# Three stage borders of an encoder layer re-ordered on one core: the first rows, gate/up and down

## The chip, the core and the metric

The kernel runs on one core of a Trainium2 chip. The metric is the device time of one execution in microseconds (us). A core has five engines that run side by side, each through its own list of instructions in order: TensorE (PE in the rows; PEld is its weight load), VectorE (DVE), ScalarE (ACT), GpSimd (POOL) and SyncE (SP), which here only issues transfers (DMA). They wait for each other by semaphores. SBUF is the core's working memory; PSUM, with eight banks of 128 x 512 float32, is where TensorE puts its sums.

## The reference

One layer on 2048 tokens of width 1024, all in float32, then a last RMSNorm:

```python
u = rms_norm(x, norm_mix_g)
q, k, v, b, c, h = split(u @ w_in)              # six parts, 512 wide each
att = diff_attention(q, k, v) + T5 bias         # softmax(s0) - lam * softmax(s1), times v; 4 heads
att = rms_norm(att, subln_g) * (1 - lam_init)
conv = b * short_conv(c * h, conv_w)            # centred, 3 wide
x = x + concat(att, conv) @ w_out
z = rms_norm(x, norm_ffn_g)
hid = silu(z @ w_gate) * (z @ w_up)             # 2816 wide
out = rms_norm(x + hid @ w_down, final_g)
```

The bias of a score depends only on key position minus query position, by 32 buckets, so that one vector of 512 values a head holds all of it.

## The kernel before

Every large product is made of three products of rounded parts: each operand is split into a high part (a rounded copy, made by ACT) and a low part (the rest, made by DVE as a subtraction of two tiles), and PE sums hi x hi, hi x lo and lo x hi. The stages follow one another on PE:

1. **The start.** The 2048 rows come in four blocks of 512 (`sb`), each of four tiles of 128 (`j`). For a tile: `square` on ACT (L745), `mean` on DVE, a power on GpSimd (L682) for 1/sqrt, `scale_x` on DVE (L1084), eight transposes on PE (`turn_u`, L1555), then `split_u` on ACT (L756) and DVE (L1090). Before that PE makes the bias vectors of the four heads (L1538), and ACT copies them out and stores them. `first_product(sb, r)` is 24 matmuls (L1546) for one of three output pieces. Between the first products of a block the next block's tiles are turned. An exponential for lambda (`lam_exp`, L782) stands on ACT ahead of the squares of block 1.
2. **The projections**, then the convolution: for each group of 128 channels three pieces `r` of four blocks.
3. **The attention.** Before its first score is used, ACT fills `window` with the bias: `fill_far` (L836) writes the constant ends and `fill_near` (L832) the middle, which SP loads (`near_stage`, L452).
4. **The output projection**, 16 row tiles `n` in `ORDER`. A tile is normed, turned into `z_turned`, copied to `zt` by ACT (`evacuate_z`, L921), and stored to a DRAM tensor `z_blocks`; for each pair of tiles four sums are made on DVE (`sum_z`, L1328 to L1333) and stored as well (`store_z`, seven stores of 256 KB, L533 and L536).
5. **Gate/up.** A Strassen-like scheme of 7 products (`k` = 0 to 6) over 4 x 4 tiles, in 44 steps: 22 chunks of weights for the first half of the tokens, then 22 for the second. A product is 12 matmuls (L1734; in step 0 L1750). The tokens' parts lie in seven pairs `z_slot[k]`, loaded from `z_blocks` and split by ACT (L928, L932) and DVE (L1314, L1320), 128 x 2048 each. `split_w` splits the weights (L943, L1354); `make_u_2`, `make_u_3`, `make_c_22`, `make_c_21` and `make_c_12` (L1360) read the sums out of PSUM; `hidden` (L1386) gives 128 x 512 of the result, stored by `store_hid` (L586). In the last step of the first half (`gate_up_step(F_CHUNKS - 1, ...)`) all seven pairs are made anew: a raw block waits in one of three `z_stage`, and SP loads block `k` (`load_z_next`, L594) when block `k - 3` has been split. `load_z_next(6)` stands on SP behind `store_hid` of that step's first piece.
6. **Down**, four groups of 22 chunks (L1792), each chunk a hidden tile and a weight tile that are loaded (L640, L642), split by ACT (L1029, L1031) and DVE (L1481, L1484). Ahead of the load of chunk 2 SP issues the four `y_rows` of the group (L634) and the gain.

All orders are written out by hand, and all SP transfers go out on one queue.

## Time and profile before

| | us |
|---|---|
| median of 3 runs | 2781.87 (2779.66 to 2782.27) |
| the profiled execution | 2779.97 |
| its span, first to last instruction | 2778.1 |
| PE busy | 2665.7 (96%) |
| DVE busy | 1511.9 (54%) |
| ACT busy | 1021.9 (37%) |
| GpSimd busy | 501.2 (18%) |

PE is the bound: what it doesn't do between its first and its last instruction is 112 us, spread over the borders between stages and over the attention. The mean granted clock of TensorE over the span was 0.988. In the chain of work that ended last, PE's gate/up and down products take 15% and 17% of the span by themselves.

### The profile page before, as it was taken

The numbers are of one execution on the slowest core, as the hardware profiler recorded it, in microseconds if no ns is written. First come the engines' busy times: TensorE is split into PE (matmuls) and PEld (weight loads), VectorE is DVE, ScalarE is ACT, GpSimd is POOL, SyncE is SP. The second block draws the span as 40 slices with busy tenths as digits, with TensorE's granted clock in tenths as the row PEclk, the third lists the DMA queues.
The fourth block names the chain that finished last, engine by engine and source line by source line (L and its number), as shares of the span: only waits on it lengthen the run. The fifth ranks groups of instructions, "written<-read, shape, count | busy, mean of one in ns | idle before, by whom it ended". The sixth has DMA issues, their size and how long they took to land. (4 is left out here: it accounts for less than half of the span.)

```text
span 2778.1 us, 34594 instructions
## 1 busy us (share of the span) xinstructions
PE 2665.7 (96%) x12280; PEld 2184.4 (79%) x12280; DVE 1511.9 (54%) x2203; ACT 1021.9 (37%) x1429; POOL 501.2 (18%) x343
## 2 busy tenths in 40 slices
PE   7999999979999999989989999989999999999997
PEld 5788888857777777778868888878888878888886
DVE  5311122258878887854466666676666643434343
ACT  5210000047667676742243333343333323323232
POOL 1000000047777777720000000000000000000000
PEclk9999999999999999999989999999999999999999
DMA  5542111223131221047762222252222235556563
GB/s 171 147 124 87 57 38 38 61 64 71 28 75 46 68 57 31 20 157 224 229 219 76 83 91 72 87 174 91 72 87 88 75 120 152 170 175 207 146 203 116
DMA packets 257359, 298.29 MB, mean 107 GB/s; under 512 B 15200, under 2 KB 175456, under 8 KB 257280
## 3 DMA queue, kind: packets, MB, share of 16 engines
q1 hardware_dynamic: 254400, 287.83, 35.1%
q0 software_dynamic: 2304, 8.39, 0.7%
q8 instruction: 46, 0.75, 0.1%
q10 hardware_dynamic: 576, 1.05, 0.1%
q14 instruction: 33, 0.27, 0.0%
HBM read 212.28 MB, written 84.93 MB: 107 GB/s over the span
## 5 line engine op out<-in xcount | busy, mean ns | idle before, releaser
L1734 PE MATMUL banks<-z_hi,w_hi 128*128 128x512 f32 x1204 | 469.9, 390 | 8.4 <-ACT p L947 5.5
L1734 PE MATMUL banks<-z_hi,w_lo 128*128 128x512 f32 x1204 | 469.4, 390 | 0.0
L1734 PE MATMUL banks<-z_lo,w_hi 128*128 128x512 f32 x1204 | 469.3, 390 | 0.0
L1546 PE MATMUL projected<-u_t_hi,w_part_hi 128*128 128x512 f32 (+1 forms) x768 | 300.3, 391 | 5.3 <-DVE u_t_lo L1090 2.6
L1546 PE MATMUL projected<-u_t_lo,w_part_hi 128*128 128x512 f32 (+1 forms) x768 | 299.3, 390 | 0.0
L1546 PE MATMUL projected<-u_t_hi,w_part_lo 128*128 128x512 f32 (+1 forms) x768 | 299.3, 390 | 0.0
L697 POOL TENSOR_TENSOR exp<-exp,exp 128x2048 f32<-128x2048 f32 x64 | 295.6, 4618 | 5.3
L1734 PEld LDWEIGHTS banks<-z_hi,w_hi 128*128 128x128 f32 x1204 | 226.8, 188 | 56.8 <-issue 5.9
L1734 PEld LDWEIGHTS banks<-z_lo,w_hi 128*128 128x128 f32 x1204 | 226.8, 188 | 47.0
L1734 PEld LDWEIGHTS banks<-z_hi,w_lo 128*128 128x128 f32 x1204 | 226.6, 188 | 47.2
L842 ACT ACTIVATE exp<-exp,neg_max 128x2048 f32<-128x2048 f32 x128 | 257.3, 2010 | 15.3 <-DVE neg_max L1228 14.4
L726 POOL TENSOR_TENSOR y_rstd<-y_mean,neg_half 128x1 f32<-128x1 f32 x16 | 8.7, 546 | 1343.4 <-DVE y_mean L1496 1343.4
L943 ACT ACTIVATE w_hi<-w_sum 128x512 fp32r<-128x512 f32 x176 | 111.3, 633 | 319.1 <-PE banks L1734 307.3
L1792 PE MATMUL banks<-down_hi,hid_hi 128*128 128x512 f32 x704 | 217.7, 391 | 3.9 <-DVE down_lo L1484 3.9
L1792 PE MATMUL banks<-down_lo,hid_hi 128*128 128x512 f32 x704 | 217.7, 390 | 0.0
L1792 PE MATMUL banks<-down_hi,hid_lo 128*128 128x512 f32 x704 | 217.4, 390 | 0.0
L852 ACT ACTIVATE a_t_hi<-tile_turned 128x512 fp32r<-128x512 f32 x256 | 148.7, 601 | 158.1 <-PE tile_turned L1622 157.8
L1240 DVE TENSOR_TENSOR a_t_lo<-tile_turned,a_t_hi 128x512 fp32r<-128x512 f32 x256 | 172.1, 687 | 54.3 <-ACT a_t_hi L852 54.2
L1604 PE MATMUL scores<-k_sum,q_part_hi 128*128 128x512 f32 x512 | 179.4, 432 | 18.7 <-DVE half_min L1228 10.3
L1481 DVE TENSOR_TENSOR hid_lo<-hid_raw,hid_hi 128x512 fp32r<-128x512 f32 x88 | 60.9, 693 | 247.6 <-ACT hid_hi L1029 247.6
L1228 DVE CUSTOM_DVE_ANT_0 exp<-scores,window,half_min 128x1024 f32<-128x1024 f32 x128 | 163.9, 1280 | 31.7 <-PE scores L1604 26.1
L1029 ACT ACTIVATE hid_hi<-hid_raw 128x512 fp32r<-128x512 f32 x88 | 55.6, 632 | 324.2 <-PE banks L1792 313.4
(143 smaller groups left out, 4420.9 us busy)
## 6 DMA issues: line engine op xcount, KB each, us to landing
down_raw<-in_w_down SPq DMA_DIRECT2D x88, 512.0 KB, 4.4
gate_raw<-in_w_gate SPq DMA_DIRECT2D x44, 512.0 KB, 4.7
up_raw<-in_w_up SPq DMA_DIRECT2D x44, 512.0 KB, 5.6
hidden_t<-hid_stage SPq DMA_DIRECT2D x88, 256.0 KB, 2.7
hid_raw<-hidden_t SPq DMA_DIRECT2D x88, 256.0 KB, 3.7
w_raw<-in_w_in SPq DMA_DIRECT2D x24, 512.0 KB, 5.3
projected_t<-stage SPq DMA_DIRECT2D x48, 256.0 KB, 2.5
z_stage<-z_blocks SPq DMA_DIRECT2D x11, 1024.0 KB, 5.8
```

The lines of the kernel that those rows point to most:

```text
L697: nc.gpsimd.tensor_tensor(exp_0[:, slot_0], exp_0[:, slot_0], exp_1[:, slot_1], ALU.add).then_inc(mixed_ready, 1)
L842: nc.scalar.activation(rows, rows, ACT.Exp, scale=-1.0, bias=neg_max[:, t % 2, part:part + 1], accum_out=exp_sum[:, part, t % 16:t % 16 + ...
L852: nc.scalar.activation(dst, turned_bank(h, t, index), ACT.Copy).then_inc(group_hi, 1)
L943: nc.scalar.activation(w_slot[k][0][:, :, :], src, ACT.Copy).then_inc(w_hi_ready_2, 1)
L1029: nc.scalar.activation(hid_part[slot][0][:, :], hid_raw[:, slot], ACT.Copy).then_inc(f_hi_ready, 1)
L1228: nc.vector.tensor_tensor_reduce(out=rows[:, half * HALF:(half + 1) * HALF], in0=scores[:, unit % 2], in1=window[:, window_slice(t, half)] ...
L1240: nc.vector.tensor_tensor(parts[1][at], turned_bank(h, t, index), parts[0][at].bitcast(FP32), ALU.subtract).then_inc(group_lo, 1)
L1481: nc.vector.tensor_tensor(hid_part[slot][1][:, :], hid_raw[:, slot], hid_part[slot][0][:, :].bitcast(FP32), ALU.subtract).then_inc(f_lo_re ...
L1546: last = nc.tensor.matmul(projected[:, bank * BANK:(bank + 1) * BANK], w_part[w][:, r, kt], u_t[u][:, kt, rows], start=(kt == 0 and n == 0 ...
L1604: last = nc.tensor.matmul(scores[:, unit % 2, b * BANK:(b + 1) * BANK], q_part[n][:, (t // 4) % 2, part, t % 4 * P:(t % 4 + 1) * P], k_sum ...
L1734: last = nc.tensor.matmul(c_bank[BANK_OF[k]], w_slot[k][w][:, kt], z_slot[k][z][:, kt], start=(kt == 0 and t == 0 and k in (0, 1, 3, 4)), ...
L1792: last = nc.tensor.matmul(y_banks[j][:, c * BANK:(c + 1) * BANK], hid_part[slot][h][:, j * P:(j + 1) * P], down_part[slot][w][:, c * BANK: ...
```

## The change

- **Start.** SP issues all four tiles of block 0 at once: two go to `x_tile`, two to `early`, which are parts of the last block's columns of `u_t_lo`, in pieces of 512 bytes. The small loads and the gain go out on ACT's queue. PE makes bias 0 first, bias 1 behind the four turns, and biases 2 and 3 behind `first_product(0, 0)`; `turn_u(1, 0)` follows those.
- **Attention.** SP loads the bias's middle right behind the start, and ACT fills the window when four products of the convolution are still to come; the high parts of the weights lie in other slots (`HI_SLOT`).
- **Gate/up.** GpSimd makes the four sums of the last two pairs, and `z_lo` of block 5 in the first half and of blocks 1, 3 and 5 in the second (`Z_ON_POOL`). SP issues the loads of blocks 4 to 6 and the last rows ahead of `store_z(6)`. PSUM banks, the places of several tiles and the orders on ACT and DVE are other.
- **Down.** DVE splits chunk 0 ahead of `make_c_12`, and ACT splits chunk 1 ahead of `silu_second`.

```diff
         lam_exp = placed(210144, "lam_exp", [P, 2])
 
+        early_rows = placed(20480 + 65536, "early_rows", [P, KT, SEQ])
+        early = [early_rows[:, :, 3 * BANK + n * P:3 * BANK + (n + 1) * P] for n in range(4)]
+        bias_vec = [early[2 + h // 2][:, 4 * (h % 2):4 * (h % 2) + 4] for h in range(HEADS)]
+
+        HI_SLOT = (1, 2, 0)
...
+
+        Z_ON_POOL = ((5,), (1, 3, 5))
+
+        def z_count(half, k, on_pool):
+
+            return sum((j in Z_ON_POOL[n]) == on_pool for n in range(half + 1) for j in range(7 if n < half else k + 1))
+
+        def wait_z(engine, half, k):
+            if k in Z_ON_POOL[half]:
+                engine.wait_ge(z_lo_pool, z_count(half, k, True))
+            else:
+                engine.wait_ge(z_lo_ready, z_count(half, k, False))
+
...
-            load_x(0, 0)
-            load_x(0, 1)
-            sp.dma_start(onehot[:, :], bucket_onehot).then_inc(rel_loaded, 16)
-            sp.dma_start(rel_sb[:, :], rel_bias).then_inc(rel_loaded, 16)
-            sp.dma_start(mix_gain[:, :], norm_mix_g[0:1, :].to_broadcast([P, D])).then_inc(gain_loaded, 16)
-            load_weights(0, 0, 0)
-            load_x(0, 2)
-            load_weights(0, 1, P)
-            load_x(0, 3)
-            load_weights(0, 2, 2 * P)
+            for j in range(2):
+                sp.dma_start(x_tile[:, j], x_rows[j * P:(j + 1) * P, :]).then_inc(x_loaded[j], 16)
+            for j in range(2):
+                sp.dma_start(early[j], x_rows[(2 + j) * P:(3 + j) * P, :].rearrange("p (k q) -> p k q", q=P)).then_inc(early_loaded[j], 16)
+            for r in range(3):
+                load_weights(0, r, r * P)
...
+            sp.wait_ge(bias_stored, 16 * HEADS)
+            load_near(0)
...
+                if n % 2 == 0 and 2 <= n < N_ROWS - 2:
                     store_z(n // 2 - 1)
                 if n == N_ROWS - 1:
 
@@ -570,6 +588,8 @@
                     for k in (4, 5, 6):
                         sp.dma_start(z_slot[k][1][:, :, :].bitcast(FP32), z_dram[0, k].rearrange("k p t -> p k t")).then_inc(z_placed[k - 4], 16)
                 store_rows(n)
+                if n == N_ROWS - 1:
...
-                sp.wait_ge(z_lo_ready, 7 + k - 2)
+                if k >= 3:
+                    wait_z(sp, 1, k - 3)
+                elif k == 0:
+                    wait_z(sp, 0, 3)
                 sp.wait_ge(z_stored[1], 16 * 28)
-                sp.wait_ge(rows_stored[k % 2], 16 * (N_ROWS // 2))
...
 
-            for n in range(N_ROWS):
+            def sum_z(pair):
+                pool.wait_ge(zt_ready, 2 * pair + 2)
+                pool.wait_ge(z_stored[(pair - 1) // 4], 16 * 7 * ((pair - 1) % 4 + 1))
+                b11, b21, b12, b22 = zt[:, 0, 0:4], zt[:, 0, 4:8], zt[:, 1, 0:4], zt[:, 1, 4:8]
+                t1, t2, t3, t4 = (zt_sum[:, n] for n in range(4))
+                nc.gpsimd.tensor_tensor(t1, b12, b11, ALU.subtract).then_inc(zt_sum_ready, 1)
+                nc.gpsimd.tensor_tensor(t3, b22, b12, ALU.subtract).then_inc(zt_sum_ready, 1)
+                pool.wait_ge(zt_sum_ready, 4 * pair + 1)
+                nc.gpsimd.tensor_tensor(t2, b22, t1, ALU.subtract).then_inc(zt_sum_ready, 1)
+                pool.wait_ge(zt_sum_ready, 4 * pair + 3)
+                nc.gpsimd.tensor_tensor(t4, b21, t2, ALU.subtract).then_inc(zt_sum_ready, 1)
+
+            def split_z(half, k):
+                pool.wait_ge(z_hi_ready, 7 * half + k + 1)
+                raw = z_stage[k % 3][:, :, :] if half else z_slot[k][1][:, :, :].bitcast(FP32)
+                nc.gpsimd.tensor_tensor(z_slot[k][1][:, :, :], raw, z_slot[k][0][:, :, :].bitcast(FP32), ALU.subtract).then_inc(z_lo_pool, 1)
+
+
+            for n in range(N_ROWS - 1):
                 rsqrt_row(n)
+            sum_z(N_ROWS // 2 - 2)
+            rsqrt_row(N_ROWS - 1)
+            for k in Z_ON_POOL[0]:
+                split_z(0, k)
+            sum_z(N_ROWS // 2 - 1)
+
+            for k in Z_ON_POOL[1]:
+                split_z(1, k)
...
+            act.dma_start(rel_sb[:, :], rel_bias).then_inc(rel_loaded, 16)
+            act.dma_start(onehot[:, :], bucket_onehot).then_inc(rel_loaded, 16)
+            act.dma_start(mix_gain[:, :], norm_mix_g[0:1, :].to_broadcast([P, D])).then_inc(gain_loaded, 16)
+            for j in range(4):
+                square(0, j)
+            keep_bias(0)
+            split_u(0, 0)
+            split_u(0, 1)
             split_weights(0, 0)
-            for j in range(4):
-                split_u(0, j)
-                if j < 2:
-                    square(0, j + 2)
-                    split_weights(0, j + 1)
+            split_u(0, 2)
+            split_u(0, 3)
+            keep_bias(1)
+            split_weights(0, 1)
+            split_weights(0, 2)
+            keep_bias(2)
+            keep_bias(3)
             act.wait_ge(lam_summed, 2)
             nc.scalar.activation(lam_exp[:, :], lam_sum[:, :], ACT.Exp).then_inc(lam_exped, 1)
...
-            act.wait_ge(piece_ready, 12 * QKV_TRIPLES + 12 * CONV_GROUPS)
+
+            act.wait_ge(piece_ready, 12 * QKV_TRIPLES + 12 * CONV_GROUPS - 4)
             act.wait_ge(w_lo_ready, 3 + 24)
+            fill_near(0)
             fill_far(0, 1)
-            fill_near(0)
             fill_far(0, 0)
...
+                if n == N_ROWS - 1:
+
+                    act.wait_ge(o_summed, N_ROWS)
+                    split_z(0, 3, 0, 4)
                 square_rows(n)
                 if n + 2 < N_ROWS:
                     split_m(n + 2)
-                if n >= 1:
+                if 1 <= n < N_ROWS - 1:
                     evacuate_z(n - 1)
...
-
-            act.wait_ge(o_summed, N_ROWS)
-            split_z(0, 3, 0, 4)
-            split_w(0, 0, 3, True)
             copy_p_0(0)
-            split_w(0, 0, 4, True)
+            for k in range(3, 7):
+                split_w(0, 0, k, True)
+            split_placed_z(4)
+            evacuate_z(N_ROWS - 2)
+            split_placed_z(5)
             evacuate_z(N_ROWS - 1)
+            split_placed_z(6)
 
             act.wait_ge(rows_stored[0], 16 * (N_ROWS // 2))
             act.wait_ge(rows_stored[1], 16 * (N_ROWS // 2))
-            for k in range(5, 7):
-                split_w(0, 0, k, True)
-            split_placed_z(4)
-            split_placed_z(5)
+            silu_first(0)
             split_w(1, 1, 0)
             split_w(1, 1, 1)
-            split_placed_z(6)
-
-            act.wait_ge(z_stored[1], 16 * 28)
-            silu_first(0)
             for k in range(2, 7):
                 split_w(1, 1, k)
             silu_second(0)
...
             split_down(0, 0, 0, False)
+            split_down(0, 1, 1, False)
             silu_second(STEPS - 1)
-            act.wait_ge(product_ready, 7 * STEPS)
-            split_down(0, 1, 1, False)
...
+            mean(0, 0)
             dve.wait_ge(gain_loaded, 16)
-            norm_block(0, lambda r: split_weights(0, r))
+            scale_x(0, 0)
+            mean(0, 1)
+            scale_x(0, 1)
+            mean(0, 2)
+            mean(0, 3)
+            scale_x(0, 2)
+            split_u(0, 0)
+            scale_x(0, 3)
+            split_u(0, 1)
+            split_weights(0, 0)
+            split_u(0, 2)
+            split_u(0, 3)
+            split_weights(0, 1)
+            split_weights(0, 2)
...
+                if n == N_ROWS - 1:
+                    split_z(0, 3, 0)
                 norm_rows(n)
-                if n % 2 == 0 and n >= 2:
+                if n % 2 == 0 and 2 <= n < N_ROWS - 2:
                     sum_z(n // 2 - 1)
...
-            split_z(0, 3, 0)
+            make_u_2(0)
             split_w(0, 0, 3)
-            make_u_2(0)
-            for k in range(4, 7):
-                split_w(0, 0, k)
+            split_w(0, 0, 4)
             split_placed_z(4)
-            sum_z(N_ROWS // 2 - 1)
+            split_w(0, 0, 5)
             make_u_3(0)
-            split_placed_z(5)
+            split_w(0, 0, 6)
+            split_placed_z(6)
+            make_c_22(0)
             sum_weights(1, 1, 0)
             split_w(1, 1, 0)
-            make_c_22(0)
             split_w(1, 1, 1)
-            split_placed_z(6)
             sum_weights(1, 1, 1)
             split_w(1, 1, 2)
 
-            dve.wait_ge(z_stored[1], 16 * 28)
+            dve.wait_ge(rows_stored[0], 16 * (N_ROWS // 2))
+            dve.wait_ge(rows_stored[1], 16 * (N_ROWS // 2))
...
-            gate_up_step(F_CHUNKS - 1, 1, lambda k: split_z(1, k, k % 3))
+            gate_up_step(F_CHUNKS - 1, 1, lambda k: None if k in Z_ON_POOL[1] else split_z(1, k, k % 3))
...
             hidden(STEPS - 1, 0)
+            split_down(0, 0, 0)
             make_c_12(STEPS - 1)
             hidden(STEPS - 1, 1)
-            split_down(0, 0, 0)
             split_down(0, 1, 1)
...
+
+            pe.wait_ge(rel_ready, 1)
+            spread_bias(0)
+            pe.wait_ge(identity_ready, 3)
             for j in range(4):
                 turn_u(0, j)
+            spread_bias(1)
+            pe.wait_ge(bias_out, 2)
+            first_product(0, 0)
+            spread_bias(2)
+            spread_bias(3)
+            turn_u(1, 0)
+            turn_u(1, 1)
+            pe.wait_ge(bias_out, 4)
+            first_product(0, 1)
+            turn_u(1, 2)
+            turn_u(1, 3)
             pe.wait_ge(bias_out, 2 * HEADS)
-            with pe.Fori(0, SB - 1) as sb:
+            first_product(0, 2)
+            with pe.Fori(1, SB - 1) as sb:
...
-            pe.wait_ge(zt_ready, N_ROWS - 1)
+            pe.wait_ge(rows_added, N_ROWS)
```

ACT at the start, where the biases are copied out (`stage<-projected`, in the changed kernel `early_rows<-projected`) and the lambda exponential is made. Before:

```order
L771 ACTIVATE bias_edges<-projected 128x2
L774 DMA bias_vectors<-stage 128x512
L739 ACTIVATE w_part_hi<-w_raw 128x1024
L756 ACTIVATE u_t_hi<-u_turned 128x8x128
L745 ACTIVATE conv_y,sumsq<-x_tile 128x1024
L739 ACTIVATE w_part_hi<-w_raw 128x1024
L756 ACTIVATE u_t_hi<-u_turned 128x8x128
L745 ACTIVATE conv_y,sumsq<-x_tile 128x1024
L739 ACTIVATE w_part_hi<-w_raw 128x1024
L756 ACTIVATE u_t_hi<-u_turned 128x8x128 x2
L782 ACTIVATE lam_exp<-lam_sum 128x2
L745 ACTIVATE conv_y,sumsq<-x_tile 128x1024 x2
```

Changed:

```order
L788 ACTIVATE w_part_hi<-w_raw 128x1024 x2
L823 ACTIVATE early_rows<-projected 128x4x128
L824 ACTIVATE bias_edges<-projected 128x2
L826 DMA bias_vectors<-early_rows 512x1x128
L823 ACTIVATE early_rows<-projected 128x4x128
L824 ACTIVATE bias_edges<-projected 128x2
L826 DMA bias_vectors<-early_rows 512x1x128
L845 ACTIVATE lam_exp<-lam_sum 128x2
L801 ACTIVATE conv_y,sumsq<-x_tile 128x1024 x2
L817 ACTIVATE stage<-projected 128x512
```

The copies of biases 2 and 3 have moved from the front of the list to right ahead of the exponential and of block 1's two squares.

SP at the end of the output projection (`z_lo` are the loads of blocks 4 to 6, `z_blocks<-zt` and `z_blocks<-zt_sum` the stores of a pair). Before:

```order
L533 DMA z_blocks<-zt 128x4x128 x3
L536 DMA z_blocks<-zt_sum 128x4x128 x4
L527 DMA rows_x<-rows 128x1024
L571 DMA z_lo_103<-z_blocks 128x4x512
L571 DMA z_lo_105<-z_blocks 128x4x512
L571 DMA z_lo_107<-z_blocks 128x4x512
L527 DMA rows_x<-rows 128x1024
L554 DMA gate_raw_158<-in_w_gate 128x8x128
L554 DMA up_raw_160<-in_w_up 128x8x128
L533 DMA z_blocks<-zt 128x4x128 x3
L536 DMA z_blocks<-zt_sum 128x4x128 x4
```

Changed:

```order
L545 DMA rows_x<-rows 128x1024
L589 DMA z_lo_104<-z_blocks 128x4x512
L589 DMA z_lo_106<-z_blocks 128x4x512
L589 DMA z_lo_108<-z_blocks 128x4x512
L545 DMA rows_x<-rows 128x1024
L551 DMA z_blocks<-zt 128x4x128 x3
L554 DMA z_blocks<-zt_sum 128x4x128 x4
L572 DMA gate_raw_159<-in_w_gate 128x8x128
L572 DMA up_raw_161<-in_w_up 128x8x128
L551 DMA z_blocks<-zt 128x4x128 x3
L554 DMA z_blocks<-zt_sum 128x4x128 x4
```

The seven stores of pair 6 have moved behind the three loads and the last rows. On ACT the copy into `zt` that waits for them now stands between the high parts of blocks 4 and 5 (`z_hi_103`, `z_hi_105`):

```order
L995 ACTIVATE z_hi_103<-z_lo_104 128x2048
L984 ACTIVATE zt<-banks 128x1024
L995 ACTIVATE z_hi_105<-z_lo_106 128x2048
L984 ACTIVATE zt<-banks 128x1024
L995 ACTIVATE z_hi_107<-z_lo_108 128x2048
L1015 ACT_TABLE_LOAD
L1015 ACTIVATE silu_156<-banks 128x512
```

Before, it stood ahead of all three. GpSimd from the last pairs' sums on, before:

```order
L700 TENSOR_TENSOR head_rstd<-head_mean,neg_half 128x4 x2
L716 TENSOR_TENSOR row_rstd<-row_mean,neg_half 128x1 x16
L726 TENSOR_TENSOR y_rstd<-y_mean,neg_half 128x1 x4
L730 DMA out<-y_rows 128x1024 x4
L726 TENSOR_TENSOR y_rstd<-y_mean,neg_half 128x1 x4
```

Changed:

```order
L739 TENSOR_TENSOR row_rstd<-row_mean,neg_half 128x1
L756 TENSOR_TENSOR z_lo_106<-z_lo_106,z_hi_105 128x2048
L746 TENSOR_TENSOR zt_sum<-zt 128x512
L747 TENSOR_TENSOR zt_sum<-zt 128x512
L749 TENSOR_TENSOR zt_sum<-zt,zt_sum 128x512
L751 TENSOR_TENSOR zt_sum<-zt,zt_sum 128x512
L756 TENSOR_TENSOR z_lo_98<-z_stage_149,z_hi_97 128x2048
L756 TENSOR_TENSOR z_lo_102<-z_stage_148,z_hi_101 128x2048
L756 TENSOR_TENSOR z_lo_106<-z_stage_150,z_hi_105 128x2048
```

The last three of these are blocks 1, 3 and 5 of the second half; DVE's list has lost the same three (of the first kernel's rows `z_lo_97`, `z_lo_101` and `z_lo_105`). DVE at blocks 1 and 2 of that step in the changed kernel:

```order
L1386 TENSOR_TENSOR z_lo_96<-z_stage_148,z_hi_95 128x2048
L1432 TENSOR_TENSOR u_152<-banks,p_151 128x512
L1426 TENSOR_TENSOR w_lo_137<-w_sum,w_hi_136 128x512
L1419 TENSOR_TENSOR w_sum<-gate_raw_158,up_raw_160 128x512
L1421 TENSOR_TENSOR w_sum<-gate_raw_158,w_sum 128x512
L1426 TENSOR_TENSOR w_lo_139<-gate_raw_158,w_hi_138 128x512
L1386 TENSOR_TENSOR z_lo_100<-z_stage_150,z_hi_99 128x2048
L1432 TENSOR_TENSOR u_153<-banks,u_152 128x512
L1426 TENSOR_TENSOR w_lo_141<-w_sum,w_hi_140 128x512
```

Between blocks 0 and 2 stand four instructions of 128 x 512 that read two tiles of SBUF (`w_lo_137`, the two `w_sum`, `w_lo_139`); `u_153`, for which the sixth product waits, follows block 2.

## Rows read from the trace of the kernel before

**Rows 1.** The page: busy time, share of the span, instructions, by engine.

```profile
PE 2665.7 (96%) x12280; PEld 2184.4 (79%) x12280; DVE 1511.9 (54%) x2203; ACT 1021.9 (37%) x1429; POOL 501.2 (18%) x343
```

**Rows 2.** Waits of PE: awaited engine and line; total us, times, longest.

```profile
PE banks L1734 <- ACT p L947: 5.5, 1, 5.5
...
PE banks L1750 <- DVE z_lo L1320: 5.3, 1, 5.3
...
PE banks L1792 <- DVE down_lo L1484: 3.9, 1, 3.9
```

**Rows 3.** Timeline of PE at the start (start, us, instruction, idle before).

```profile
7.38 7.19 PE L1538 MATMUL projected<-onehot,rel_wide 32*128 32x512 f32 x8 [7.38 <-DVE rel_wide L1067]
...
25.84 1.97 PE L1555 MATMUL u_turned<-identity,u_tile 128*128 128x128 f32 x8 [1.55 <-DVE u_tile L1084]
...
30.38 0.79 PE L1546 MATMUL projected<-u_t_hi,w_part_hi 128*128 x1 [2.58 <-DVE u_t_lo L1090]
...
37.33 1.91 PE L1555 MATMUL u_turned<-identity,u_tile 128*128 128x128 f32 x16
...
39.00 0.48 PE L1546 MATMUL projected<-u_t_hi,w_part_hi 128*128 x1
...
44.54 1.03 PE L1555 MATMUL u_turned<-identity,u_tile 128*128 128x128 f32 x8
```

**Rows 4.** Timeline of ACT at the start.

```profile
30.50 0.20 ACT L782 ACTIVATE lam_exp<-lam_sum 128x2 f32<-128x2 f32 x1 [1.64 <-DVE lam_sum L1131]
```

**Rows 5.** Timelines of DVE and POOL there, two squares later.

```profile
32.02 0.55 POOL L682 TENSOR_TENSOR rstd<-mean_eps,neg_half 128x1 f32<-128x1 f32 x1 [9.06 <-DVE mean_eps L1077]
...
33.09 1.27 DVE L1084 SCALAR_TENSOR_TENSOR u_tile<-x_tile,rstd,mix_gain 128x1024 f32<-128x1024 f32 x1
...
33.26 1.52 POOL L682 TENSOR_TENSOR rstd<-mean_eps,neg_half 128x1 f32<-128x1 f32 x1 [0.69 <-DVE mean_eps L1077]
```

**Rows 6.** The page: the long GpSimd additions of the attention.

```profile
L697 POOL TENSOR_TENSOR exp<-exp,exp 128x2048 f32<-128x2048 f32 x64 | 295.6, 4618 | 5.3
```

**Rows 7.** Timelines of ACT and DVE where the attention begins.

```profile
577.23 0.52 ACT L832 ACTIVATE window<-near_stage 128x384 f32<-128x384 f32 x1 [3.77 <-DMA near_stage<-bias_vectors]
...
577.79 1.23 DVE L1228 CUSTOM_DVE_ANT_0 exp<-scores,window 128x1024 f32<-128x1024 f32 x1 [4.48 <-ACT window L832]
```

**Rows 8.** Timelines of SP, ACT and PE where gate/up begins.

```profile
1409.86 2.57 SPq L571 DMA_DIRECT2D z_lo<-z_blocks  x3
...
1425.05 0.63 ACT L943 ACTIVATE w_hi<-up_raw 128x512 fp32r<-128x512 f32 x1 [7.03 <-issue]
...
1446.31 0.47 PE L1734 MATMUL banks<-z_hi,w_hi 128*128 128x512 f32 x1
```

**Rows 9.** Engines and transfers in that stretch (the windows view).

```profile
1404.00:1424.00 20.00, 16.73 (x68) 13.05 (x68) 10.54 (x13) 7.22 (x9) 1.08 (x2) 0.83 1.06 356
```

**Rows 10.** Timelines of DVE, PE, SP and ACT between the halves.

```profile
1837.69 2.28 DVE L1314 TENSOR_TENSOR z_lo<-z_stage,z_hi 128x2048 fp32r<-128x2048 f32 x1
...
1843.43 0.50 PE L1734 MATMUL banks<-z_hi,w_hi 128*128 128x512 f32 x1 [2.47 <-DVE u L1360]
...
1850.33 0.69 DVE L1386 TENSOR_TENSOR hid_stage<-up,silu 128x512 f32<-128x512 f32 x1
...
1851.51 0.37 SPq L594 DMA_DIRECT2D z_stage<-z_blocks  x1
...
1857.77 1.91 ACT L928 ACTIVATE z_hi<-z_stage 128x2048 fp32r<-128x2048 f32 x1 [7.16 <-DMA z_stage<-z_blocks]
```

**Rows 11.** Timelines of SP, ACT, DVE and PE where the down product begins.

```profile
2279.66 1.87 SPq L634 DMA_DIRECT2D y_rows<-rows_x  x4
...
2290.73 0.63 ACT L1029 ACTIVATE hid_hi<-hid_raw 128x512 fp32r<-128x512 f32 x1 [10.75 <-DMA hid_raw<-hidden_t]
...
2293.03 1.23 DVE L1484 TENSOR_TENSOR down_lo<-down_raw,down_hi 128x1024 fp32r<-128x1024 f32 x1 [0.88 <-ACT down_hi L1031]
...
2294.41 0.64 PE L1792 MATMUL banks<-down_hi,hid_hi 128*128 128x512 f32 x2
```

More of the change, by code:

```diff
@@ L113, in build @@
         x_loaded = [sem(f"x_loaded_{i}") for i in range(2)]
+        early_loaded = [sem(f"early_loaded_{i}") for i in range(2)]
         w_hi_ready = sem("w_hi_ready")
@@ L1083, in scale_x @@
                     dve.wait_ge(turned, 4 * sb + j + 1)
-                nc.vector.scalar_tensor_tensor(u_tile[:, j % 2], x_tile[:, j % 2], rstd[:, j:j + 1],
-                                               mix_gain[:, :], ALU.mult, ALU.mult).then_inc(u_ready, 1)
+                scaled_x, rows, gain = u_tile[:, j % 2], x_tile[:, j % 2], mix_gain[:, :]
+                if isinstance(sb, int) and sb == 0 and j >= 2:
+                    scaled_x, rows, gain = scaled_x.rearrange("p (k q) -> p k q", q=P), early[j - 2], gain.rearrange("p (k q) -> p k q", q=P)
+                nc.vector.scalar_tensor_tensor(scaled_x, rows, rstd[:, j:j + 1], gain, ALU.mult, ALU.mult).then_inc(u_ready, 1)
             def split_u(sb, j):
@@ L1535, in _, with spread_bias @@
             pe.sem_inc(turned, 2)
-            pe.wait_ge(rel_ready, 1)
-            for h in range(HEADS):
+            def spread_bias(h):
                 nc.tensor.matmul(projected[:, h * BANK:(h + 1) * BANK], rel_wide[:, h], onehot[:, :],
                                  start=True, stop=True).then_inc(bias_mm, 1)
-            pe.wait_ge(identity_ready, 3)
             def product(bank, r, rows):
```

81 lines of the change are left out of this document (39 added, 42 removed).

## The prediction

> **What bounds the kernel now.** I read the page's busy shares first: PE is busy for 2665.7 of 2778.1 us [rows 1], so a gain can only come out of the 112 us in which it isn't, or out of its clock. Then the waits of PE: three single waits of 5.5, 5.3 and 3.9 us stand at the borders that the change touches [rows 2]. Then the timelines there. The first product starts at 30.38 and ends at 37.33, when the next block's tiles are ready to be turned; the second starts at 39.00 [rows 3]. The attention's first score waits 4.48 us on DVE for ACT's window, and ACT waited for the load of its middle [rows 7]. Gate/up comes into its loop at 1446.31 [rows 8], after a stretch with a granted clock of 0.83 and the transfers full at 356 GB/s [rows 9]. Between the halves block 6 arrives late [rows 10], and down starts against its own third chunk [rows 11]. So there are five places, and each is one term.
>
> **1. The start.** Chain of the four tiles, now without a second round of loads: the four tiles, the gain and one weight are 3 MB; at 356 GB/s [rows 9], I put the gain's landing near 7 us and the first scaled tile at 9.5. Behind it DVE has three more scalings (1.27 each, [rows 5]), four low parts and one weight's, which I take at the same size: 8 x 1.2 = 9.7, and some 3 us in which it waits for a turn (1.97, [rows 3]) and ACT's copy (1.0). The first product then starts at about 22.2, 8.2 ahead of 30.38, and ends at E = 29.2 if it needs its 6.95 us again. But the eight turns behind it no longer find their tiles. Biases 2 and 3 now stand behind this product on PE: 7.19 us for 8 instructions [rows 3] is 0.9 each; the same kind of instruction shows half speed there (8 turns in 1.97 against 16 in 1.91 at 37.33), so at full speed the two biases take 1.8. ACT copies them (some 1 us for the second, with its store's issue), then comes the lambda exponential at E + 3.0, then the squares. From the exponential to the end of the first scaling it is 33.09 + 1.27 - 30.50 = 3.9 us [rows 4, 5]; the second is scaled behind the power's end at 34.78, so 1.3 later, at 36.05, or 5.6 behind the exponential. Its turn ends at E + 8.6 + 1 to 2 = 38.8 to 39.8, against 39.00. The 8 us are given back here, and PE has idled for 5 us, behind which products run at half clock for a while (the 0.83 over 20 us of rows 9 is such a stretch and cost 3.4 us). The next load of x hangs on the first scaling, at E + 6.9 = 36.1 instead of 34.4. I take +1.5; from -2 (E at 26, clock kept) to +4 (the 512-byte pieces load slowly).
>
> **2. The attention's entry.** The window is written under products, whose engine has nothing to do with it; ACT idles there. The wait of 4.48 goes [rows 7]; late next is the score itself, about 0.4 us behind the last convolution piece. With PE no longer idle, its scores 3 and 4 aren't slowed: a few tenths more. I take -4.6, from -3.5 to -5.5. What hangs behind moves with it: the stores of the last convolution piece have to land before score 3, with some 1 us to spare.
>
> **3. Gate/up's entry.** The three loads of blocks 4 to 6 (1 MB each) go out when the projection ends, 4 us ahead of 1409.86 [rows 8]. But the copy of tile 14 into `zt`, which waits for the stores of pair 6, now stands ahead of block 5's high part on ACT, and these stores (7 x 256 KB) have moved behind the loads and the last rows. The transfers are full and go in line: the last rows, issued at 1412.5 behind the loads, held ACT until 1425.05 (the wait put down to "issue", [rows 8]). The same bytes in another order: the line's last member ends when it did, so the stores land at about 1425.0. Then 1.0 for the copy, 1.9 for block 5's high part (as in [rows 10]) and its low part on GpSimd. That is an addition of 128 x 2048, 4.62 us [rows 6]: 1432.6. Products 0 to 4 are done by then; 5 and 6 follow, 12 matmuls each of some 0.227 (24 take 5.5 from 39.00 to 44.54, [rows 3]), the first twelve and a few more at half clock (1.2 GHz), 8.5 in all: 1441.1 against 1446.31. I take -5.3; from -3 to -13, the latter if the stores overtake the loads, since block 5 is then ready when PE wants it.
>
> **4. Between the halves.** DVE loses three low parts of 2.28 [rows 10], GpSimd gets them at 4.62 [rows 6]. PE waited 2.47 us for a sum behind two of them, which would go. It doesn't count if DVE is otherwise free: product 2 of the new half waits for a copy on ACT behind block 6's high part, whose load SP issues at 1851.51, behind the store of the piece that DVE makes at 1850.33 [rows 10]. That piece comes behind block 4, which comes behind block 1's low part. With GpSimd's 4.62 in place of DVE's, which can start at 1835.5, block 1 ends at 1840.1, where DVE ended it at 1839.97 [rows 10], so without any hindrance this term is 0.
> But GpSimd and DVE hinder each other when both read. Row: the power takes GpSimd 0.55 us, and 1.52 when DVE has started a scaling (two tiles read from SBUF) 0.17 earlier [rows 5]; 1.52 is the 1.1 of the scaling's rest and 0.45. In the attention GpSimd's 64 additions take 4.62 beside DVE, whose instructions there take one operand from PSUM [rows 6, 7]. What the row shows one way I expect the other way: who has started keeps the second reader out to its end. Then: GpSimd takes block 1 at 1835.5, when its high part is there, and DVE's next weight part waits until 1840.1. Four instructions of 128 x 512 (0.6) and block 2 (2.2) end at 1844.9, and the sum for product 5 at 1845.4, 2.0 behind 1843.43. GpSimd takes block 3 at 1844.8, to 1849.4; DVE's next weight part stands, and block 4 ends at 1853.4. GpSimd takes block 5, to 1858.0, and the piece behind (0.69, two SBUF tiles) ends at 1858.7 instead of 1851.0. Its store and the load of block 6 go out 7.6 us later, and so does everything behind 1857.77. Bounds 0 and +9; I take +7.6, since the one row there is on it shows full exclusion.
> The Trainium skill (SBUF — State Buffer, section "Who interferes with whom") says the same of both directions: a DVE instruction with two SBUF inputs contends with a GpSimd instruction that reads SBUF, and whoever starts first blocks the other for the whole instruction. By that rule the term is +7.6; this trace agrees for GpSimd's side (0.55 to 1.52) and shows nothing of DVE's.
>
> **5. Down's entry.** DVE has chunk 0 ready 3.3 us earlier, and PE's wait of 3.9 [rows 2] shrinks to 0.6. But chunk 2 was only just in time: its low part ends at 2294.3, and PE takes it at 2294.41 without a wait [rows 11]. Its load stands behind the four `y_rows` from 2279.66 on, 2 MB, and landed at 2290.73. They in turn stand behind the store of the last hidden piece, which the two low parts (0.6 and 1.2) put ahead of `make_c_12` push back by 0.6. So PE is done with chunks 0 and 1 at 2288.7 (48 x 0.227 from 2277.8), waits 6 us, and starts chunk 2 at 2294.9, now at half clock for some 5 us: -0, +0.5 and +2.2, so +2.7, from 0 to +3.5.
>
> Sum: +1.5 - 4.6 - 5.3 + 7.6 + 2.7 = +1.9 us. On the profiled execution's 2779.97 (span 2778.1 and 1.9 around it) that is 2781.9; the median of the runs is 1.9 above it, so 2783.8. 0.2% of the median is 5.6 us, about what a measurement of this kernel tells from no change.
>
> **The rivals.**
> - *No exclusion the other way.* DVE reads on beside GpSimd, term 4 is 0: 2783.8 - 7.6 = 2776.2. For it: 4.62 beside a DVE that is busy for most of the attention; against it: those DVE instructions read one SBUF tile, and the 1.52.
> - *The stores of pair 6 overtake the loads.* Then block 5 is ready when PE comes to it, and term 3 is -13: 2783.8 - 7.7 = 2776.1. Against it: the last rows' 12.6 us behind the same loads [rows 8].
> - *Slower: the first rows come late.* The early tiles travel in 512-byte pieces beside the gain and the weights. If they take twice the 1.5 us each that 356 GB/s gives, E is 3 later, everything to the second product hangs on E (term 1), and the first projection's later turns with it: +4 in place of +1.5, and with term 5 and term 4 at their upper ends (0.8 and 1.4 more), 2788.5. It decides once E is beyond 31.
> - *The work moved to GpSimd does what it says, and PE's clock stays up at all five borders:* rival one and terms 1 and 5 at their lower ends, -3.5 and -2.7: 2770.
>
> **How the numbers follow.** Forecast 0.45, of which faster by 0.2% 0.04, within 0.33, slower 0.08. No exclusion 0.24: 0.13 faster, 0.11 within, since 2776.2 lies on the bound. Overtaking 0.10: 0.06 and 0.04. Late rows 0.14, all slower. Everything well 0.07, faster. Faster 0.30, same 0.48, slower 0.22. The range leaves out half of the last case and the ends of the slow one: 2771 to 2790; the forecast's own is 2779 to 2789.
>
> **What would show it.** Term 1: the first product near 22, a wait of some 5 us on PE for `u_tile` behind biases 2 and 3, and the second product near 39 all the same. Term 2: no wait for the window. Term 3: ACT waits for a store (`z_blocks<-zt_sum`) near 1425 and PE for GpSimd's `z_lo`, about 10 us. Term 4: DVE instructions with two SBUF inputs that last 3 to 5 us or start late beside GpSimd's 4.62, and block 6's load behind them; were DVE's rows there 0.69 and 2.28 as before, rival one is true. Term 5: a PE wait of 6 us at chunk 2 instead of 3.9 at chunk 0. The forecast is wrong if PE finds its tiles behind the first product, or if block 5 is split before 1425.

## The result and the profile after

| | before | after |
|---|---|---|
| median of 20 runs, us | 2777.98 (2775.04 to 2782.27) | 2783.48 (2778.42 to 2785.10) |
| the profiled execution | 2779.97 | 2783.90 |
| its span | 2778.1 | 2782.1 |

The ratio is 1.0019, with a 95% interval of 1.0013 to 1.0025: slower by 0.13 to 0.25%, with the point estimate just inside the 0.2% that I called no change. The forecast was 2783.8. That it is met to 0.3 us is partly luck: I added 1.9 to a level of 2781.87, and the median of 20 runs of before is 3.9 lower. The honest comparison is of differences: 1.9 forecast, 3.9 between the two profiled executions, 5.5 between the medians. The profiled execution of before is 2.0 above its median and that of after 0.4 above, so some 1.6 of the 5.5 stand in neither trace.

The page's busy times say nothing of this; PE is even busy for less [rows 1]:

```profile
PE 2664.3 (96%) x12280; PEld 2182.8 (78%) x12280; DVE 1514.3 (54%) x2191; ACT 1021.5 (37%) x1429; POOL 536.9 (19%) x355
```

The waits of PE do [rows 2] (awaited engine and line; total us, times, longest):

```profile
PE banks L1822 <- ACT p L1010: 9.6, 2, 8.8
PE banks L1838 <- issue: 9.5, 1, 9.5
PE u_turned L1627 <- DVE u_tile L1147: 9.1, 4, 5.5
...
PE banks L1880 <- DVE down_lo L1557: 6.1, 2, 5.6
PE banks L1822 <- DVE u L1432: 4.3, 1, 4.3
```

Single waits of 8.8, 9.5, 5.5, 5.6 and 4.3 stand where 5.5, 5.3, 3.9 and 2.5 stood before: the waits have not gone, they have moved.

To see what each place is worth, compare one instruction of the steady stretch behind it in both traces. Two such pairs, before and after: the first long addition on GpSimd behind the attention's entry, then the silu of the last but one gate/up step, behind the border between the halves.

```profile
588.61 4.55 POOL L697 TENSOR_TENSOR exp<-exp,exp 128x2048 f32<-128x2048 f32 x1
...
2247.23 0.60 ACT L952 ACTIVATE silu<-banks 128x512 f32<-128x512 f32 x1 [2.09 <-PE banks L1734]
```

```profile
587.13 4.54 POOL L720 TENSOR_TENSOR exp<-exp,exp 128x2048 f32<-128x2048 f32 x1
...
2248.54 0.60 ACT L1015 ACTIVATE silu<-banks 128x512 f32<-128x512 f32 x1 [2.09 <-PE banks L1822]
```

At 587 us after is 1.48 early, at 2248 it is 1.31 late. Read so at every border:

| place (term) | after minus before, in the steady stretch behind it | the term: difference to the row above | predicted |
|---|---|---|---|
| start (1) | +3.23 (a convolution piece, 117.01 against 113.78) | +3.2 | +1.5 |
| attention's entry (2) | -1.60 (12 tiles of the output projection, all alike) | -4.8 | -4.6 |
| gate/up's entry (3) | -5.45 (19 steps of the first half, all alike) | -3.9 | -5.3 |
| between the halves (4) | +1.30 (20 steps of the second half) | +6.8 | +7.6 |
| down's entry (5) | +3.97 (all chunks from the seventh on) | +2.7 | +2.7 |
| sum | | +4.0 | +1.9 |

These are single executions, one of each kernel. Kernels whose code is the same up to a border differ there as well: by up to 1.3 us in the output projection, and at gate/up's entry, where the transfers decide, the term lay between -1.8 and -4.3 in the six traces that have this entry unchanged (after and the first, second, fourth, fifth and eighth experiment). Term 4 is steadier: 6.0 to 7.3 in the five traces that have GpSimd's part there unchanged.

**The start** [rows 3 to 5], rows of PE, ACT and DVE:

```profile
30.81 1.98 PE L1611 MATMUL projected<-onehot,rel_wide 32*128 32x512 f32 x4
38.27 3.54 PE L1627 MATMUL u_turned<-identity,u_tile 128*128 128x128 f32 x16 [5.48 <-DVE u_tile L1147]
41.56 0.48 PE L1618 MATMUL projected<-u_t_hi,w_part_hi 128*128 128x512 f32 x1
```

```profile
34.35 0.20 ACT L845 ACTIVATE lam_exp<-lam_sum 128x2 f32<-128x2 f32 x1 [0.53 <-ACT bias_edges L824]
```

Biases 2 and 3 follow the first product at 30.81, ACT comes to the exponential at 34.35, and the first turn waits 5.48 us for its tile. The second product starts at 41.56 (before 39.00).

**The attention's entry** [rows 7]. The first score on DVE waits 0.60 for PE; the wait of 4.48 for the window is gone.

```profile
577.15 1.23 DVE L1300 CUSTOM_DVE_ANT_0 exp<-scores,window 128x1024 f32<-128x1024 f32 x1 [0.60 <-PE scores L1692]
```

**Gate/up's entry** [rows 8]: the copy of tile 14 on ACT waits for the stores of pair 6, block 5 is made behind it on ACT and GpSimd, and PE waits 9.53 for it.

```profile
1423.90 1.02 ACT L984 ACTIVATE zt<-banks 128x1024 f32<-128x1024 f32 x1 [10.38 <-DMA z_blocks<-zt_sum]
1424.83 1.90 ACT L995 ACTIVATE z_hi<-z_lo 128x2048 fp32r<-128x2048 f32 x1
```

```profile
1426.80 4.51 POOL L756 TENSOR_TENSOR z_lo<-z_lo,z_hi 128x2048 fp32r<-128x2048 f32 x1 [15.61 <-ACT z_hi L995]
```

```profile
1431.41 0.76 PE L1838 MATMUL banks<-z_hi,w_hi 128*128 128x512 f32 x1 [9.53 <-issue]
...
1439.84 0.39 PE L1822 MATMUL banks<-z_hi,w_hi 128*128 128x512 f32 x1
```

"issue" names nobody here. GpSimd's row ends at 1431.31, 0.1 ahead of the matmul, and the matmul reads the block that it writes, so I take it as the releaser; the third experiment bears that out.

**Between the halves** [rows 10], DVE, then GpSimd in the same 20 us, then SP and PE behind them. These are the rows that decide the case:

```profile
1830.43 4.73 DVE L1426 TENSOR_TENSOR w_lo<-w_sum,w_hi 128x512 fp32r<-128x512 f32 x1
...
1836.89 2.28 DVE L1386 TENSOR_TENSOR z_lo<-z_stage,z_hi 128x2048 fp32r<-128x2048 f32 x1
...
1839.69 4.46 DVE L1426 TENSOR_TENSOR w_lo<-w_sum,w_hi 128x512 fp32r<-128x512 f32 x1
...
1844.68 0.67 DVE L1426 TENSOR_TENSOR w_lo<-w_sum,w_hi 128x512 fp32r<-128x512 f32 x1
1845.28 2.28 DVE L1386 TENSOR_TENSOR z_lo<-z_stage,z_hi 128x2048 fp32r<-128x2048 f32 x1
...
1848.24 4.33 DVE L1458 TENSOR_TENSOR hid_stage<-up,silu 128x512 f32<-128x512 f32 x1
```

```profile
1829.99 4.63 POOL L756 TENSOR_TENSOR z_lo<-z_stage,z_hi 128x2048 fp32r<-128x2048 f32 x1 [390.30 <-ACT z_hi L991]
1838.38 5.22 POOL L756 TENSOR_TENSOR z_lo<-z_stage,z_hi 128x2048 fp32r<-128x2048 f32 x1 [3.77 <-ACT z_hi L991]
1846.99 5.03 POOL L756 TENSOR_TENSOR z_lo<-z_stage,z_hi 128x2048 fp32r<-128x2048 f32 x1 [3.39 <-ACT z_hi L991]
```

```profile
1853.05 0.39 SPq L616 DMA_DIRECT2D z_stage<-z_blocks  x1
```

```profile
1862.10 0.76 PE L1822 MATMUL banks<-z_hi,w_hi 128*128 128x512 f32 x1 [8.83 <-ACT p L1010]
```

The same DVE instruction takes 0.67 alone and 4.73 if GpSimd's began 0.44 earlier: it ends some 0.55 behind GpSimd's, so it has stood still until about then. The same shows the other way round: GpSimd's second and third row begin while a low part of DVE (2.28) is under way, 0.8 and 0.6 ahead of its end, and last 5.22 and 5.03 instead of some 4.6. The load of block 6 goes out at 1853.05 (before 1851.51, with PE 5.45 us ahead), and PE waits 8.83 at 1862.10.

**Down's entry** [rows 11]:

```profile
2279.01 0.73 PE L1880 MATMUL banks<-down_hi,hid_hi 128*128 128x512 f32 x2 [0.59 <-DVE down_lo L1557]
2295.74 1.22 PE L1880 MATMUL banks<-down_hi,hid_hi 128*128 128x512 f32 x2 [5.55 <-DVE down_lo L1557]
```

The wait at chunk 0 is 0.59 (before 3.91), the one at chunk 2 is 5.55 (before none).

### The profile page after: what moved, and what is told of

It reads as the page before. It is cut to its first block and busy times, and to the rows that moved or that the text cites. A ratio compares the mean times of both kernels' runs of the same rounds, so it can differ in the third digit from the quotient of the medians.

```text
span 2782.1 us, 34570 instructions
## 1 busy us (share of the span) xinstructions
PE 2664.3 (96%) x12280; PEld 2182.8 (78%) x12280; DVE 1514.3 (54%) x2191; ACT 1021.5 (37%) x1429; POOL 536.9 (19%) x355
```

## The experiments

All times are medians, ratios are to the kernel before on the same chip. "Back" is against the changed kernel, by the difference of the ratios (1.0019 minus the ratio, times 2778); by the intervals of the two ratios such a difference is known to some 3 us, and to 4 or more in the experiments from the fifth on. Each kernel was timed beside the kernel before, whose median was 2778.43 in the first four, 2779.15 in the next four and 2777.43 in the last two.

**1. The blocks between the halves on DVE again.**

```diff
-        Z_ON_POOL = ((5,), (1, 3, 5))
+        Z_ON_POOL = ((5,), ())
```

> The changed kernel, but the low parts of blocks 1, 3 and 5 between the halves are made by DVE again. Theory (GpSimd and DVE shut each other out when both read two SBUF tiles): in the trace of the changed kernel the stretch between the halves costs 6.75 us against before (the silu copies stand 5.45 us early ahead of it and 1.30 late behind it), and three DVE instructions of 0.68 last 4.73, 4.46 and 4.33 beside GpSimd's additions. With DVE alone these rows are 0.68 again, block 6 is loaded some 5 to 7 us earlier, PE's longest wait there is 5.5 instead of 8.8 and its wait of 4.3 is 2.5; the time falls by 6.8 us. Rival (the place is as late for another reason, the three loads that SP issues or the order on ACT): DVE's rows get short but PE's waits stay, and less than 3 us come back.

2776.66 us, ratio 0.9995 (0.9986 to 1.0004): 6.7 back. In its trace the stretch between the halves costs 8.3 us less than in after (and 1.5 less than in before), PE's waits there are 2.47 and 4.08, and DVE's rows are short:

```profile
1839.60 0.69 DVE L1426 TENSOR_TENSOR w_lo<-w_sum,w_hi 128x512 fp32r<-128x512 f32 x1
...
1846.67 0.69 DVE L1458 TENSOR_TENSOR hid_stage<-up,silu 128x512 f32<-128x512 f32 x1
```

So the loss of term 4 came from GpSimd's part; the rival is out. Reckoned from the steady stretch ahead of it, block 6's load goes out 7.0 later in after than in before, and in this run when it did in before.

**2. The squares ahead of biases 2 and 3** (ACT).

```diff
-            keep_bias(2)
-            keep_bias(3)
             act.wait_ge(lam_summed, 2)
             nc.scalar.activation(lam_exp[:, :], lam_sum[:, :], ACT.Exp).then_inc(lam_exped, 1)
+            square(1, 0)
+            square(1, 1)
+            keep_bias(2)
+            keep_bias(3)
...
-                square(sb + 1, 0)
-                square(sb + 1, 1)
+                if not first:
+                    square(sb + 1, 0)
+                    square(sb + 1, 1)
```

> The changed kernel, but on ACT the lambda exponential and the squares of tiles 0 and 1 of block 1 stand ahead of the copies of biases 2 and 3. Theory (PE's wait of 5.48 us behind the first product hangs on the exponential, which hangs on the biases, which hang on the product): the squares run before 30 us, the turns follow the biases at once, the wait of 5.5 and that of 1.0 go, PE's clock stays up, and the second product starts at 34 to 35 instead of 41.56; the time falls by 6 to 8 us. Rival (the tiles of block 1 are not loaded by then, or the copies of biases 2 and 3, now behind the squares, hold the third product): the second product starts no earlier than 38 and at most 3 us come back.

2777.47 us, ratio 0.9996 (0.9987 to 1.0005): 6.4 back. The exponential runs at 27.44, inside the first product; the 16 turns follow the biases at 32.76 without a wait, and the second product starts at 34.48, 7.1 earlier. The wait of 5.5 was the order on ACT, as the prediction had it.

```profile
32.76 1.97 PE L1630 MATMUL u_turned<-identity,u_tile 128*128 128x128 f32 x16
34.48 0.47 PE L1621 MATMUL projected<-u_t_hi,w_part_hi 128*128 128x512 f32 x1
```

**3. Blocks 4 to 6 ahead of the copies of tiles 14 and 15** (ACT).

```diff
-            split_placed_z(4)
-            evacuate_z(N_ROWS - 2)
-            split_placed_z(5)
-            evacuate_z(N_ROWS - 1)
-            split_placed_z(6)
+            for k in (4, 5, 6):
+                split_placed_z(k)
+            evacuate_z(N_ROWS - 2)
+            evacuate_z(N_ROWS - 1)
```

> The changed kernel, but on ACT the high parts of blocks 4, 5 and 6 stand ahead of the two copies of tiles 14 and 15, the first of which waits 10.4 us for the stores of pair 6. Theory (PE's 9.5 us ahead of product 5 are this wait, then 1.9 for the high part and 4.5 on GpSimd): ACT makes block 5 as soon as it has landed, near 1415, GpSimd has it near 1420, and PE goes from product 4 to 5 without a wait; its clock stays up, so the loop starts near 1428 instead of 1439.8. Some of it is lost to the next wait, since the stores of the rows still land near 1424: I expect 7 to 10 us less in the time. Rival (the loads of the blocks themselves land only near 1422, with the stores, because all transfers share one bandwidth): product 5 starts at 1428 or later and at most 4 us are won.

2775.70 us, ratio 0.9992 (0.9983 to 1.0001): 7.5 back, of which the trace shows 4.8 at this border (after's own -3.9 there is 0.5 better than the mean of the six traces, so the edit may be worth a little more), 1.1 ahead of it, where the code is the same, and 1.3 behind. ACT makes block 5 at 1415.10; product 5 waits 0.49 instead of 9.53. But the loop starts at 1433.50, not near 1428, behind a new wait:

```profile
1423.01 0.47 PE L1837 MATMUL banks<-z_hi,w_hi 128*128 128x512 f32 x1 [0.49 <-DVE u L1431]
...
1433.50 0.79 PE L1821 MATMUL banks<-z_hi,w_hi 128*128 128x512 f32 x1 [4.08 <-DVE w_lo L1425]
```

Ahead of it stand the next weights (`up_raw` landed at 1428.6) and, again, GpSimd; how much of the 4.08 belongs to each isn't separated. One weight part on DVE took 5.11 beside GpSimd's 4.62, and the weight sums took 1.5 to 1.8 instead of 0.69 beside the last pair's sums.

```profile
1417.15 5.11 DVE L1425 TENSOR_TENSOR w_lo<-up_raw,w_hi 128x512 fp32r<-128x512 f32 x1
...
1431.69 1.75 DVE L1425 TENSOR_TENSOR w_lo<-gate_raw,w_hi 128x512 fp32r<-128x512 f32 x1
```

**4. Chunks 2 and 3 ahead of the residual's rows** (SP; DVE's wait for the gain moves to group 1).

```diff
             store_hid(1, STEPS - 1, F_CHUNKS - 1, 0)
+            load_down(0, 2, 0)
             store_hid(1, STEPS - 1, F_CHUNKS - 1, 1)
+            load_down(0, 3, 1)
             sp.wait_ge(product_ready, 7 * STEPS)
             load_y_rows(0)
...
-            with sp.Fori(1, F_CHUNKS // 2) as pair:
+            with sp.Fori(2, F_CHUNKS // 2) as pair:
...
-            dve.wait_ge(out_gain_loaded, 16)
             for group in range(4):
+                if group == 1:
+                    dve.wait_ge(out_gain_loaded, 16)
```

> The changed kernel, but SP loads chunks 2 and 3 of the down product ahead of the four rows of the residual, and DVE waits for the gain only ahead of the second group. Theory (PE's wait of 5.6 us at chunk 2 is the 2.5 MB ahead of its load): chunk 2 is split near 2286, PE doesn't wait behind chunk 1, the clock stays up; the 5.6 go and some 2.5 of half clock: the time falls by 7 to 8 us. Rival (the load of chunk 4, now behind the rows, is late instead): a wait of 3 us or more at chunk 4, and less than 4 us are won.

2775.38 us, ratio 0.9989 (0.9980 to 0.9998): 8.3 back, 8.4 at this border in the trace. Chunk 2's low parts end at 2286.6 and PE runs through; its only wait in down is 0.6. The load of chunk 4 comes late on ACT (a wait of 1.30) but not for PE.

**5. Block 6 loaded ahead of the step's first store** (SP, on top of the first experiment).

```diff
+            load_z_next(6)
             store_hid(0, F_CHUNKS - 1, F_CHUNKS - 1, 0)
-            load_z_next(6)
```

> The kernel of the first experiment (blocks 1, 3 and 5 on DVE again), and SP loads block 6 ahead of the store of the step's first hidden piece instead of behind it. Theory (PE's longest wait there, 4.1 us in that experiment, hangs on this load, which stood behind DVE's piece at 1847.4): the load goes out when block 3 is split, near 1842.5, PE's wait of 4.1 goes and with it some 2 us of half clock: 5 to 6 us less than the first experiment, so 2771. Rival (the transfers are the limit there: the loads of blocks 4 and 5 end only near 1845): block 6 lands near 1850 instead of 1853.5 and 3 us are won at most.

2768.47 us, ratio 0.9968 (0.9956 to 0.9980). The block's high part starts at 1845.11 instead of 1853.52, PE's long wait is gone and this border costs 6.1 less than in the first experiment, 7.7 less than in the kernel before. By the ratios it is 7.5 faster than the first experiment, known to 4 us, so the 5 to 6 that I expected fit, and so does the trace's 6.1. The rival's 3 us don't fit the trace.

**6. All five edits together.**

> All five edits at once: squares ahead of biases 2 and 3, blocks 4 to 6 ahead of the copies of tiles 14 and 15, the blocks between the halves on DVE, block 6 loaded first, chunks 2 and 3 ahead of the rows. If the five borders are independent, the gains add up: against the changed kernel 6.9 + 6.1 + 7.9 + 8.2 from the medians and 5.5 for block 6, 35 in all, so near 2749; against the kernel before, near 0.989. If they aren't (a stage that starts earlier finds its loads late), less: 2755.

2749.19 us, ratio 0.9898 (0.9883 to 0.9913); expected 2749. By the ratios the five edits bring 36.4 one by one and 33.6 together, which is the same within the interval of 0.3%. A steady stretch of some 380 us or more stands between each two borders. It beats both kernels.

**7. GpSimd with one operand.** This kernel leaves out the subtraction in GpSimd's low parts of blocks 5, 1, 3 and 5.

```diff
-  nc.gpsimd.tensor_tensor(z_slot[k][1][:, :, :], raw, z_slot[k][0][:, :, :].bitcast(FP32), ALU.subtract).then_inc(z_lo_pool, 1)
+  nc.gpsimd.tensor_scalar(z_slot[k][1][:, :, :], raw, 1.0, None, ALU.mult).then_inc(z_lo_pool, 1)
```

> The changed kernel, but GpSimd makes its low parts of blocks 5 (first half), 1, 3 and 5 (second half) from one tile: it multiplies the raw block by one instead of subtracting the high part, so this leaves the subtraction out. Theory A (what shuts DVE out is a GpSimd instruction with two operands from SBUF): GpSimd's instructions get shorter and DVE's weight parts beside them last 0.68 again; 5 to 7 us less. Theory B (any GpSimd instruction that reads SBUF shuts out a DVE instruction with two SBUF operands): DVE's rows still last as long as what is left of GpSimd's, near 4 us if it needs as long for one operand as for two.

A single run, so its time (2780.47) says little; in its trace this border costs 4.0 against before, where after has 6.8. DVE and GpSimd between the halves:

```profile
1829.89 3.75 DVE L1426 TENSOR_TENSOR w_lo<-w_sum,w_hi 128x512 fp32r<-128x512 f32 x1
...
1838.17 3.52 DVE L1426 TENSOR_TENSOR w_lo<-w_sum,w_hi 128x512 fp32r<-128x512 f32 x1
...
1845.79 3.52 DVE L1458 TENSOR_TENSOR hid_stage<-up,silu 128x512 f32<-128x512 f32 x1
```

```profile
1829.46 5.37 POOL L756 TENSOR_SCALAR z_lo<-z_stage 128x2048 fp32r<-128x2048 f32 x1 [390.43 <-ACT z_hi L991]
```

Theory A is out: one operand on GpSimd's side shuts DVE out as well. Theory B is nearly right: DVE is held for some 3.5 us from GpSimd's start, but goes on 1.8 ahead of the end of GpSimd's row (1834.83 against 1833.0), where with two operands it stood to the end. GpSimd's rows are rough, so where its reading ends is open.

**8. The window late.**

```diff
-            sp.wait_ge(bias_stored, 16 * HEADS)
-            load_near(0)
...
             store_conv(CONV_GROUPS - 1)
+            sp.wait_ge(bias_stored, 16 * HEADS)
+            load_near(0)
...
-            act.wait_ge(piece_ready, 12 * QKV_TRIPLES + 12 * CONV_GROUPS - 4)
+            act.wait_ge(piece_ready, 12 * QKV_TRIPLES + 12 * CONV_GROUPS)
             act.wait_ge(w_lo_ready, 3 + 24)
-            fill_near(0)
             fill_far(0, 1)
+            fill_near(0)
```

> The changed kernel, but SP loads the bias's middle and ACT fills the window where the kernel before does, behind the last piece of the convolution. Theory (term 2): the wait of 4.5 us ahead of the first exponentials comes back and with it a stretch at a lower clock, so the time rises by 4.8 us, to 2788. Rival (the load of the middle was the whole wait and has its slot earlier in the queue now): less than 2 us.

2787.53 us, ratio 1.0031 (1.0019 to 1.0044): 3.3 slower than the changed kernel by the ratios, 4.0 by the medians and at the output projection in the trace. The waits are those of before, to a tenth: ACT 3.85 for the load, DVE 4.56 for the window. With the load and the filling back in their old places the waits are back, and both hang on the load, so the rival is out by the trace; the time alone, known to 4 us, wouldn't rule it out. An early load with a late filling wasn't run.

**9 and 10. No help from GpSimd, beside all five edits once more.** Experiment 9 has the five edits, and in it DVE also makes block 5 of the first half and the sums of the last two pairs (`Z_ON_POOL = ((), ())`, `sum_z` back on DVE).

> All five edits, and GpSimd helps nowhere: DVE makes the sums of the last two pairs (the last ones behind c22 of the first step) and the low part of block 5 of the first half as well. Theory (beside DVE's subtractions GpSimd gives nothing, since each of its instructions shuts DVE out to its end): with all five edits one DVE weight part of the first step lasted 5.09 beside GpSimd's 4.62 where DVE needs 2.28 for the same block, and four more lasted 1.6 to 1.8 beside the last pair's sums. Without them PE's waits of 0.4 at products 5 and 6 go and the one of 3.5 at the loop's start shrinks to some 2: 2 us less, near 2747. Rival (GpSimd's help is worth its place ahead of the loop): DVE gets 2.3 for the block and 2 x 2.7 for the sums, the last turn and PE's waits get longer, and the time rises by 2 us or more.

> The kernel with all five edits once more, on the same chip as the one without GpSimd's help, so that the two can be compared: 0.990 of the kernel before, near 2749, its loop in gate/up entered behind a wait of 3.5 us.

2745.95 us in 9 (ratio 0.9889, 0.9872 to 0.9905) and 2748.07 in 10 (0.9899, 0.9883 to 0.9916). In 9 the waits of 0.4 at products 5 and 6 are gone, and the loop is entered behind 2.47; the medians say 2 less, but the intervals overlap, and the same entry with unchanged code waited 3.52 in the sixth and 1.68 in the tenth run, which then waits 1.91 more for a copy on ACT. So no gain from GpSimd's help shows here, and no cost either: the difference between the two kernels is known only to some 6 us.

## Why the prediction came out so

- **Term 1, the start: mechanism right, size off** (+3.2 for +1.5). The place is as predicted, and the second experiment shows that ACT's order alone makes it. What was mis-sized is E, the end of the first product: 30.8 instead of 29.2. It started at 22.77 (I said 22.2), but took 8.0 us instead of 6.95: ten of its 24 matmuls last 0.63 and all behind 27.6 last 0.39, where in before five last 0.63. The granted clock is 0.50 over the stretch (the lower level, 1.2 GHz); ahead of the product PE had waited 1.4, 1.8 and 1.3 us for its tiles. Which matmuls fall on the lower clock varies: in seven traces with this start unchanged the product takes 7.3 to 8.5 us, with 8 to 12 of them, and the term is 2.5 to 3.4. I took the 6.95 from a product of before, and priced half clock behind the 5 us wait, but not here. The slower rival's mark, E beyond 31, was missed by 0.2 without its cause: the rows came in time.

```profile
17.70:27.80 10.10, 8.97 (x22) 6.06 (x23) 6.76 (x11) 4.19 (x6) 0.00 (x0) 0.50 0.47 140
```

- **Term 2, the window: right** (-4.8 for -4.6), and the eighth experiment gives 4.2 of it back (in its trace the term is -0.6).
- **Term 3, gate/up: mechanism right, size off** (-3.9 for -5.3; -1.8 to -4.3 over the six traces). The stores held ACT until 1423.90 (I said 1425.0), product 5 came at 1431.41 (1432.6), the loop at 1439.84 (1441.1). My times are on the time axis of before, and after arrives 1.6 early, so up to the loop the sum held to 0.4: -4.9 by then. I stopped it there. Behind it PE lost 1.0 more, 0.8 of it waiting for a copy on ACT. DVE's weight parts of just then lasted 1.77 each beside GpSimd's sums of the last pair: the exclusion that I priced in term 4 had a second place, and I left it out. That it is what made the copy late is argued from the order of the instructions; no run tests it alone.
- **Term 4, the halves: right** (+6.8 for +7.6). Block 6's load went out 7.0 later, where I said 7.6. The first experiment gives back 8.3 in the trace, more than the term: without GpSimd this border is 1.5 shorter than before's, 0.6 by a shorter load of block 6 and 1.0 by fewer matmuls at the lower clock (7 against 12) behind the wait. I had put all but the exclusion at 0; single traces don't say whether that 1.5 is the change or the execution. The one row of before in which a GpSimd power lasted 1.52 beside a DVE scaling carried a rule for the other direction. By the Trainium skill (SBUF — State Buffer, section "Who interferes with whom") the one that starts first blocks the other for the whole instruction; the 4.73, 4.46 and 4.33 agree with it, the 3.5 of the seventh experiment only if GpSimd's reading ends ahead of its row. The rival without exclusion, which I gave 0.24, is out by the first experiment.
- **Term 5, down: right** (+2.7 for +2.7): 0.59 and 5.55 where I said 0.6 and 6.
- **The sum** was 2 us low in the trace and 3.6 in the medians, both inside 0.2%, but twice and nearly three times what I forecast. Terms 1 and 3 were too kind by 3.1 together and term 4 too harsh by 0.8; that the errors partly cancel, and that I started from a median 3.9 too high, is luck. Two small slips of adding (term 3 comes to -5.2, and 1844.9 in term 4 to 1844.7) change nothing.

## What to carry to other kernels

Before work is handed to GpSimd, look for instructions of DVE beside it that read two tiles from SBUF. Here each of them stood still for most or all of GpSimd's; price that, and at every place where it happens. When a wait is removed at a border, write down which load or copy is next in line on the same queue, and move that too: here four of the five borders only changed which wait they had, and four moves of one or two lines each, with the work back on DVE, brought 1.0%. Where a steady stretch lies between the borders, their gains can be measured one by one; here they added up (36.4 and 33.6).
